# Expert weights in 2 MB loads with four rows per partition; the second expert layer by two experts and both column halves

## The chip, the cores and the metric

The kernel runs on one core of one Trainium2 chip. Its time is the device time of one execution in microseconds (us), and lower is better. The engines are PE (TensorE, matrix products; its weight loads are PEld), DVE (VectorE), ACT (ScalarE), POOL (GpSimd) and SP (SyncE, which issues nearly all transfers here). Everything is float32.

## The reference

Two residual blocks on 256 tokens of width 1024. The first has four half-step feed-forward layers, two mixers and two gated projections. The second has an attention-like mixer and an expert layer, twice:

```
x = x + g1 * mixer(norm(x))                  # layer 0: also for 256 context tokens
h = norm(x) * (1 + sc2) + sh2
aff  = softmax(h @ w_router)                 # 16 experts
gate, idx = top_k(aff.T, 32)                 # each expert picks 32 tokens
xe   = h[idx]                                # 16 x 32 x 1024
hid  = silu(xe @ w1) * (xe @ w3)             # w1, w3, w2: 16 x 1024 x 1024 per layer
ye   = hid @ w2 * gate
x = x + g2 * scatter_add(ye, idx)
```

In layer 0 the same weights serve the tokens and the context, so an expert has 64 rows there, and 32 in layer 1. One expert matrix is 4 MB (MB is 2^20 bytes where it counts loads), so each expert layer reads 3 x 16 x 4 = 192 MB of weights, each byte once.

## The kernel before

Each engine has a program written out by hand, and they meet on semaphores. Only two things set the order around the change.

**The ring.** Weights go through `ring`, twelve slots of 1 MB (128 partitions x 2048 floats). SP's `load` (line 3682) waits until the slot's previous user has been released (`w_used[s]`) and issues one 1 MB transfer. PE's `chunk` waits for `w_in[s]`. `done_with_chunk` only puts the slot on a list: it is released by the next product that PE runs (`mm`, the `held.pop()`), one slot per product. The list matters: the slots of one piece of work come free when the next piece has begun. Loads are issued strictly in the order in which SP's program names them; a wait of one holds up all behind it.

**The expert layers.** `moe(l)` on each engine. Layer 0 works in 8 passes of 2 experts (`groups` = 2, 64 rows each, so a product is 128 x 64 against 128 x 512), layer 1 in 4 passes of 4 experts (`groups` = 4, 32 rows each). A pass multiplies with `w1` (name h1), `w3` (h3) and, after `turn_hidden` has transposed the hidden rows, `w2` (y, run in the next round before that round's h1 and h3); `scatter` adds the previous pass's result to its tokens. `by_weights` does one matrix of a pass: for each quarter q of the 1024 input rows it takes one 1 MB chunk per expert (two rows of 4 KB, so 8 KB, per partition), and for both rows, both column halves and all experts it runs a product; I call the work between two such waits a unit. In layer 0 a unit is 2 chunks (2 MB) and 8 products, in layer 1 it is 4 chunks (4 MB) and 16 products. The first pass of a layer is p; layer 0 then has the written-out rounds a and b, where `gather_quarter` and `gather_x` also gather tokens, and a loop of five more rounds (layer 1: two); the last y is `m0.z.y` or `m1.z.y`.

Some chunks of the first pass do not go through the ring but early into other buffers (`EARLY`: SX, H, AR, XC), as soon as these are free. `ISSUED` gives the order in which layer 0's first loads are issued: with chunks 16 and 17, which belong to m0.a.h1, ahead of the early chunks 13, 14, 7, 12 and 15, whose buffers come free late.

The last unit of `m1.z.y` is cut by column halves (`last_half`): four half chunks for the left half, `add_last(0)`, four for the right half, `add_last(1)`. While `paired(k)` picks every second column of the token rows, it matches the two rows per partition of a chunk.

## Time and profile before

| | us |
|---|---|
| median of 3 runs | 2720.47 |
| the runs | 2719.14 to 2724.95 |
| span of the profiled execution, first to last instruction | 2717.5 |
| PE busy | 2486.2 (91%) |
| DVE busy | 958.0 (35%) |
| ACT busy | 450.6 (17%) |
| chain that ended last, share on PE | 75% |
| chain that ended last, share on DMA | 20%, of it `ring<-moe_w` 19% |

The profiled execution's own device time is not listed beside its span, so the span stands for it: it lies 3.0 us under the median of the runs. The page cuts the span into 40 slices of 68 us. A product in float32 shows as two MATMUL instructions, so x16 in a row of the trace is 8 products. A matmul's duration overlaps that of its neighbours; what counts is the distance between starts.

The second block begins at about 1220 us. The first expert layer's products run from 1602 to 2053 us, the second's from 2274 us to the end.

### The profile page before, as it was taken

Reading aid. Unit: us, or ns where it says so; the run is one execution under the profiler, and the core shown is the slowest. Engines: PE = TensorE matmul, PEld = TensorE weight load, DVE = VectorE, ACT = ScalarE, POOL = GpSimd, SP = SyncE. Lnnn points to the kernel's source line nnn. Section 1 sums busy time; section 2 is a strip of 40 time slices with the busy share of each in tenths; the row PEclk is TensorE's granted clock in tenths of the full one; section 3 lists DMA queues with packets and bytes.
Section 4 is the critical chain, followed back from the end, with each engine's and each line's share of the span. In section 5 each row is a group of like instructions: output and inputs, shape, how many; then the busy total and the mean of one; then the engine's idle time right before and its main releaser. Section 6 shows DMA issues by size and latency. Waiting matters only on the chain.

```text
span 2717.5 us, 26882 instructions
## 1 busy us (share of the span) xinstructions
PE 2486.2 (91%) x10689; PEld 1408.1 (52%) x10689; DVE 958.0 (35%) x1629; ACT 450.6 (17%) x858; POOL 49.3 (2%) x63
## 2 busy tenths in 40 slices
PE   9999999999999999999999999988889998665656
PEld 4546754464548864558876654433335765221213
DVE  5452454555561454552235642111123242000002
ACT  1101311011111221112223420000002131000001
POOL 0000000000000000011000100000000000000000
PEclk9999999999999999999999999999999999888788
DMA  7458663663459564567422279999997328999998
GB/s 281 144 212 277 222 234 137 227 234 126 170 206 300 176 216 140 216 183 158 145 90 76 103 270 407 421 422 422 422 422 257 109 93 343 421 421 422 422 421 350
DMA packets 239078, 700.95 MB, mean 258 GB/s; under 512 B 16952, under 2 KB 126696, under 8 KB 192296
## 3 DMA queue, kind: packets, MB, share of 16 engines
q1 hardware_dynamic: 231776, 686.73, 66.8%
q10 hardware_dynamic: 5088, 8.33, 0.9%
q0 software_dynamic: 2112, 4.46, 0.9%
q8 instruction: 73, 1.20, 0.2%
q14 instruction: 29, 0.24, 0.0%
HBM read 695.30 MB, written 4.06 MB: 257 GB/s over the span
## 4 chain that ended last, share of the span: by engine, by line
PE 75%; DMA 20%; DVE 2%; SPq 1%; issue 1%; ACT 0%; ACTq 0%; POOL 0%; DVEq 0%
PE bank L589 73%; DMA ring<-moe_w 19%; PE bank L598 2%; SPq L3682 1%; DMA ring<-ada_w 0%; ACT AR L3013 0%; DVE AR L1904 0%; DMA AR<-vec 0%; DVE AR L1901 0%; DVE AR L2506 0%; DVE AR L2780 0%; DVE H L1904 0%; DVE AR L2888 0%; DVE AR L2779 0%; DVE XC L1907 0%
## 5 line engine op out<-in xcount | busy, mean ns | idle before, releaser
L589 PE MATMUL bank<-ring,AR 128*32 128x512 f32 (+3 forms) x3656 | 895.9, 665 | 195.8 <-DMA ring<-moe_w 188.6
L589 PEld LDWEIGHTS bank<-ring,AR 128*32 128x32 f32 (+2 forms) x3656 | 329.1, 150 | 716.5 <-issue 685.1
L589 PE MATMUL bank<-H,ring 128*128 128x256 f32 (+3 forms) x2288 | 513.6, 386 | 1.8 <-DVE H L1904 0.8
L589 PEld LDWEIGHTS bank<-H,ring 128*128 128x128 f32 (+2 forms) x2288 | 423.5, 188 | 85.4 <-issue 25.8
L3013 ACT ACTIVATE AR<-bank 128x512 f32<-128x512 f32 (+3 forms) x306 | 174.9, 576 | 1681.8 <-PE bank L589 1108.2
L589 PE MATMUL bank<-AR 128*128 128x512 f32 (+15 forms) x1456 | 402.9, 446 | 15.0 <-DVE AR L2871 6.2
L589 PE MATMUL bank<-ring,H 128*128 128x256 f32 (+3 forms) x1536 | 407.1, 500 | 1.1 <-DVE H L1904 0.6
L1901 DVE TENSOR_TENSOR AR<-AR,bank 128x512 f32<-128x512 f32 (+2 forms) x156 | 97.1, 624 | 763.5 <-PE bank L589 762.3
L589 PEld LDWEIGHTS bank<-ring,H 128*128 128x128 f32 (+1 forms) x1536 | 228.2, 170 | 153.8 <-issue 115.9
L589 PEld LDWEIGHTS bank<-AR 128*128 128x128 f32 (+7 forms) x1456 | 208.8, 184 | 161.7 <-issue 133.6
L1901 DVE TENSOR_TENSOR SX<-ring 128x1024 f32<-128x1024 f32 (+3 forms) x48 | 78.0, 1624 | 287.5 <-PE bank L589 263.6
L589 PE MATMUL bank<-SX,AR 128*128 128x512 f32 (+4 forms) x360 | 135.5, 536 | 2.4 <-ACT SX L3013 2.2
L3013 ACT ACTIVATE AR<-AR 128x512 f32<-128x512 f32 (+7 forms) x156 | 95.2, 637 | 231.5 <-DVE AR L1901 144.4
L598 PEld LDWEIGHTS bank<-cst,AR 128*128 128x128 f32 (+2 forms) x629 | 75.1, 151 | 72.5 <-issue 52.8
L1901 DVE TENSOR_TENSOR AR<-AR 128x256 f32<-128x256 f32 (+8 forms) x180 | 89.6, 526 | 52.2 <-ACT AR L3013 50.0
L598 PE MATMUL bank<-cst,AR 128*128 128x128 f32 (+2 forms) x629 | 98.0, 280 | 4.3 <-DVE AR L1901 1.4
L1913 DVE COPY AR<-bank 128x512 f32<-128x512 f32 (+4 forms) x48 | 29.0, 616 | 174.5 <-PE bank L589 148.6
L589 PEld LDWEIGHTS bank<-SX,AR 128*128 128x128 f32 (+2 forms) x360 | 58.5, 178 | 58.9 <-issue 47.0
L1901 DVE TENSOR_TENSOR ring<-ring,AR 128x1024 f32<-128x1024 f32 (+3 forms) x48 | 77.4, 1618 | 5.0 <-PE bank L589 5.0
L1901 DVE TENSOR_TENSOR ring<-ring 128x1024 f32<-128x1024 f32 (+3 forms) x48 | 77.8, 1620 | 0.5
L1901 DVE TENSOR_TENSOR AR<-ring,SX 128x1024 f32<-128x1024 f32 (+3 forms) x48 | 77.7, 1619 | 0.1
L3013 ACT ACTIVATE AR<-XC 128x512 f32<-128x512 f32 (+1 forms) x76 | 38.5, 535 | 181.1 <-DVE XC L1907 109.1
(145 smaller groups left out, 938.1 us busy)
## 6 DMA issues: line engine op xcount, KB each, us to landing
ring<-moe_w SPq DMA_DIRECT2D x364, 1024.0 KB, 15.2
ring<-ffn_w SPq DMA_DIRECT2D x104, 1024.0 KB, 9.5
ring<-ada_w SPq DMA_DIRECT2D x48, 1024.0 KB, 5.5
ring<-m_w_in SPq DMA_DIRECT2D x26, 1024.0 KB, 11.9
ring<-ffn_w SPq DMA_DIRECT2D x32, 768.0 KB, 7.6
ring<-even_w_in SPq DMA_DIRECT2D x24, 1024.0 KB, 6.4
AR<-moe_w SPq DMA_DIRECT2D x18, 512.0 KB, 7.6
ring<-m_w_out SPq DMA_DIRECT2D x8, 1024.0 KB, 11.5
```

The costliest lines, as they stand in the source:

```text
L589: ins = pe.matmul(o, lhsT, rhs, start=start, stop=stop, skip_group_check=True)
L598: ins = pe.transpose(o, src, ident[0:n, 0:n])
L1901: return dve.tensor_tensor(o, a, b, op)
L1913: dve.tensor_copy(o, v).then_inc(free[b], 1)
L3013: return act.activation(o, i, func, **kw)
L3682: sp.dma_start(v, src).then_inc(w_in[s], 16)
```

## The change

- SP gets `load_pair`: one transfer of 2 MB into two neighbouring slots (an even one and the next), with four rows of 4 KB (16 KB) per partition. It waits for the release of both slots, and signals `w_in` of the even one only. `Ring.pair` skips a slot where the count is odd.
- The loads of w1 and w3 of each layer's first pass stay single 1 MB chunks (and early ones); all later loads of expert weights are pairs, but for the very last.
- Layer 0's first loads: chunks 16 and 17 are now the first pair, behind the early chunks.
- `by_weights` works in units of two experts and four rows: 2 pairs (4 MB), 16 products in both layers. In layer 1 a matrix is four units: experts 0 and 1, both halves of the input rows, then experts 2 and 3. The right column half of an expert goes to the row group two further on (`turned_place`), so that four products in a row lie in four different column groups of the array.
- Because of that, the right half's result rows of layer 1 belong to other experts than the left half's: DVE makes a second set of index and gate columns (`IC`, `GC` 4:8) and a second one-hot `PG[:, nt:2*nt]` per pass, and `scatter` and `add_last` take the one that belongs to their half.
- Rows are permuted by four in place of two: `paired` becomes `fourth` (every fourth column as a product's weights), and the `shift` rows are gathered by 16 small products in place of 4.
- The end of `m1.z.y`: experts 2 and 3 only; two single chunks, then two half chunks for the left half, `add_last(0)`, two for the right.

```diff
 class Ring:
+    def pair(self):
+        self.k += self.k % 2
+        s = self.k % RING
+        self.k += 2
+        n, before = self.uses[s], self.release[s + 1]
+        self.uses[s] += 1
+        self.release[s] = self.release[s + 1] = (s, n + 1)
+        return s, self.count(n), before
...
-        ISSUED = [(*range(7), 8, 9, 10, 11, 16, 17, 13, 14, 7, 12, 15), ()]
+        FIRST = [(*range(7), 8, 9, 10, 11, 13, 14, 7, 12, 15), tuple(range(32))]
...
+            def pair_of_chunks():
+                s, n, _ = loads.pair()
+                pe.wait_ge(w_in[s], 16 * n + 16)
+                held_next.append(s)
+                return ring[:, s:s + 2, :].rearrange("p a (k n) -> p (a k) n", n=D)
...
-                        for r in range(2):
-                            for half in range(2):
-                                mm(bank[b][64 * half:64 * half + 64, 4 * r:4 * r + 4], ident[:, r:P:2],
-                                   MODS[:, 1, 24 + half:32:2, 0], r == 0, True, full[b] if r == 1 and half == 1 else None)
+                        for r in range(4):
+                            for q in range(4):
+                                mm(bank[b][32 * q:32 * q + 32, 2 * r:2 * r + 2], ident[:, r:P:4],
+                                   MODS[:, 1, 24 + q:32:4, 0], r == 0, True, full[b] if r == 3 and q == 3 else None)
...
+                    def turned_place(g, half):
+                        return (g + 2 * half) % groups if l == 1 else g
...
-                            ws = [weights_of_pass(i) for _ in range(groups)]
-                            for kk in range(2):
-                                k = 2 * q + kk
-                                for half in range(2):
-                                    for g, (place, w) in enumerate(ws):
...
+                        units = [(first, q) for first in range(0, groups, 2) for q in range(2)]
+                        for u, (first, q) in enumerate(units):
+                            if between is not None and u in at:
+                                between(*((u,) if len(at) > 1 else ()))
+                            if name == "m1.z.y" and u == 3:
+                                ws = [(None, chunk(2, D)) for _ in range(2)]
+                                for kk in range(2):
+                                    products(4 + kk, ws, kk, first)
+                                for _ in ws:
+                                    done_with_chunk()
                                 for half in range(2):
-                                    last_half(half, b0 + half, left)
+                                    ws = [(None, chunk(2, 512)) for _ in range(2)]
+                                    for kk in range(2):
+                                        products(6 + kk, ws, kk, first, (half,))
+                                    for _ in ws:
+                                        done_with_chunk()
+                                    if half == 0:
+                                        idle_products(5)
+                                        add_last(0)
                                 continue
+                            ws = [(None, pair_of_chunks()) for _ in range(2)]
+                            for kk in range(4):
+                                products(4 * q + kk, ws, kk, first)
+                            for _ in ws:
+                                done_with_chunk()
...
                     def one_hot(n):
+                        if l == 1:
+                            dve.tensor_scalar(PG[:, nt:2 * nt], IOF[:, 0:nt], IC[:, bass.ds(n + 4, 1)], GC[:, bass.ds(n + 4, 1)],
+                                              ALU.is_equal, ALU.mult)
...
+            def load_pair(src):
+                s, n, before = loads.pair()
+                if loads.i is not None or n > 0:
+                    sp.wait_ge(w_used[s], n)
+                if before is not None and before[0] != s:
+                    sp.wait_ge(w_used[before[0]], before[1])
+                sp.dma_start(ring[:, s:s + 2, :].rearrange("p a n -> p (a n)"), src).then_inc(w_in[s], 16)
...
+            first_singles()
+            if l == 0:
+                pairs(1, (0,))
+                pairs(0, (2,))
+                pairs(1, (1, 2))
+                pairs(2, (0, 1, 2))
+            else:
+                pairs(0, (2,))
```

SP's queue where layer 0's expert weights begin, before the change. `w_usedN` is the release of ring slot N; `full2` and `full7` are the waits for the buffers H and AR:

```order
L3682 DMA ring<-moe_w3_2 128x2048 [waits w_used4]
L3682 DMA ring<-moe_w1_2 128x2048 [waits w_used5]
L3682 DMA ring<-moe_w1_2 128x2048 [waits w_used6]
L3752 DMA H<-moe_w3_2 128x1024 [waits full2]
...
L3752 DMA AR<-moe_w3_2 128x4x256 [waits full7]
L3752 DMA AR<-moe_w3_2 128x4x256
L3682 DMA ring<-moe_w1_2 128x2048 [waits w_used7]
L3682 DMA ring<-moe_w1_2 128x2048 [waits w_used8]
L3682 DMA ring<-moe_w1_2 128x2048 [waits w_used9]
```

And now:

```order
L3729 DMA ring<-moe_w3_2 128x2048 [waits w_used4]
L3809 DMA H<-moe_w3_2 128x1024 [waits full2]
...
L3809 DMA AR<-moe_w3_2 128x4x256 [waits full7]
L3809 DMA AR<-moe_w3_2 128x4x256
L3739 DMA ring<-moe_w1_2 128x4096 [waits w_used7,w_used6]
L3739 DMA ring<-moe_w1_2 128x4096 [waits w_used9,w_used8]
L3739 DMA ring<-moe_w1_2 128x4096 [waits w_used11,w_used10]
```

The two chunks that filled slots 5 and 6 ahead of the early ones are gone; slot 5 is skipped, and the first pair needs slot 7, which holds the first chunk of the layer.

PE's queue at m0.a.h1 in layer 0 (x7 stands for seven more products), before:

```order
L589 MATMUL bank<-ring,SX 64x512 [waits w_in5,free1,w_in6,free0,xcur_ready]
L589 MATMUL bank<-ring,SX 64x512 x7
L589 MATMUL bank<-ring,SX 64x512 [waits w_in8,w_in7]
L589 MATMUL bank<-ring,SX 64x512 x7
L598 MATMUL bank<-cst,AR 128x128 [waits free4,free2]
```

And now:

```order
L606 MATMUL bank<-ring,SX 64x512 [waits w_in6,free1,w_in8,free0,xcur_ready]
L606 MATMUL bank<-ring,SX 64x512 x15
L615 MATMUL bank<-cst,AR 128x128 [waits free4,free2]
L615 MATMUL bank<-cst,AR 128x128 x3
L606 MATMUL bank<-ring,SX 64x512 [waits w_in0,w_in10]
```

The boundary in the middle of the sixteen products, at which the first two slots were released, is gone.

PE's queue at the end of the kernel, before:

```order
L589 MATMUL bank<-ring,AR 32x512 [waits w_in4,w_in5,w_in3,w_in2]
L589 MATMUL bank<-ring,AR 32x512 x7
L589 MATMUL bank<-cst 128x2 [waits free5]
L589 MATMUL bank<-cst 128x2 x3
L589 MATMUL bank<-AR 128x512 [waits free6,pg_ready]
L589 MATMUL bank<-AR 128x512
L589 MATMUL bank<-ring,AR 32x512 [waits w_in8,w_in9,w_in7,w_in6]
L589 MATMUL bank<-ring,AR 32x512 x7
L589 MATMUL bank<-AR 128x512 [waits free7,pg_ready]
L589 MATMUL bank<-AR 128x512
```

And now:

```order
L606 MATMUL bank<-ring,AR 32x512 [waits w_in5,w_in4]
L606 MATMUL bank<-ring,AR 32x512 x7
L606 MATMUL bank<-ring,AR 32x512 [waits w_in7,w_in6]
L606 MATMUL bank<-ring,AR 32x512 x3
L606 MATMUL bank<-cst 128x2 [waits free5]
L606 MATMUL bank<-cst 128x2
L606 MATMUL bank<-AR 128x512 [waits free6,pg_ready]
L606 MATMUL bank<-AR 128x512
L606 MATMUL bank<-ring,AR 32x512 [waits w_in9,w_in8]
L606 MATMUL bank<-ring,AR 32x512 x3
L606 MATMUL bank<-AR 128x512 [waits free7,pg_ready]
L606 MATMUL bank<-AR 128x512
```

The left half's result (`bank<-AR 128x512`) now stands between two column halves of 1 MB each, where it stood between two of 2 MB each.

## Rows read from the trace of the kernel before

**Rows 1.** The page: slices of the span, granted clock and DMA rate
```profile
PEclk9999999999999999999999999999999999888788
GB/s 281 144 212 277 222 234 137 227 234 126 170 206 300 176 216 140 216 183 158 145 90 76 103 270 407 421 422 422 422 422 257 109 93 343 421 421 422 422 421 350
```

**Rows 2.** DMA view, four stretches: rows of 1, 2, 4 and 8 KB
```profile
DMA packets 6899, 6.97 MB, mean 349 GB/s; under 512 B 104, under 2 KB 6898, under 8 KB 6898
...
DMA packets 3492, 6.96 MB, mean 387 GB/s; under 512 B 98, under 2 KB 98, under 8 KB 3491
...
DMA packets 763, 2.93 MB, mean 418 GB/s; under 512 B 48, under 2 KB 48, under 8 KB 763
...
DMA packets 13901, 101.25 MB, mean 422 GB/s; under 512 B 1542, under 2 KB 1542, under 8 KB 1542
```

**Rows 3.** Chain of waits, one pass of layer 0: start, us, what
```profile
1847.30 10.72 PE bank L589 x32
...
1883.66 23.19 DMA ring<-moe_w
1906.99 10.72 PE bank L589 x32
```

**Rows 4.** PE in order of time, layer 0 begins, [idle before <- releaser]
```profile
1616.05 7.04 PE L589 MATMUL bank<-ring,AR 128*64 128x512 f32 x32
...
1629.78 7.04 PE L589 MATMUL bank<-ring,SX 128*64 128x512 f32 x32
1636.75 1.23 PE L598 MATMUL bank<-cst,AR 128*128 128x128 f32 x8
```

**Rows 5.** DMA by stretches of layer 0's begin (clock, share, GB/s last)
```profile
1634.00:1635.00 1.00, 1.00 (x8) 0.35 (x6) 0.00 (x0) 0.00 (x0) 0.00 (x0) 1.00 0.10 25
1635.00:1636.00 1.00, 1.00 (x8) 0.36 (x6) 0.00 (x0) 0.00 (x0) 0.00 (x0) 1.00 0.73 131
...
1640.00:1680.00 40.00, 40.00 (x192) 16.01 (x189) 8.18 (x9) 2.39 (x4) 0.00 (x0) 1.00 1.01 422
```

**Rows 6.** PE in order of time, end of round b, gather_x, next y
```profile
1727.99 3.65 PE L589 MATMUL bank<-ring,AR 128*64 128x512 f32 x16 [1.31 <-DMA ring<-moe_w]
1731.57 7.13 PE L589 MATMUL bank<-AR 128*128 128x512 f32 x16
1738.55 1.11 PE L598 MATMUL bank<-cst,AR 128*128 128x128 f32 x8
1739.50 7.08 PE L589 MATMUL bank<-AR 128*128 128x256 f32 x32
1746.51 28.98 PE L589 MATMUL bank<-ring,AR 128*64 128x512 f32 x134
```

**Rows 7.** PE in order of time, end of layer 0
```profile
2026.30 3.65 PE L589 MATMUL bank<-ring,AR 128*64 128x512 f32 x16 [1.32 <-DMA ring<-moe_w]
2029.89 7.13 PE L589 MATMUL bank<-AR 128*128 128x512 f32 x16
...
2038.80 13.96 PE L589 MATMUL bank<-ring,AR 128*64 128x512 f32 x64 [0.83 <-ACT AR L3013]
```

**Rows 8.** PE in order of time, layer 1
```profile
2397.31 5.34 PE L589 MATMUL bank<-ring,AR 128*32 128x512 f32 x32 [4.59 <-DMA ring<-moe_w]
```

**Rows 9.** PE in order of time, the kernel's end
```profile
2700.86 1.92 PE L589 MATMUL bank<-ring,AR 128*32 128x512 f32 x16 [1.77 <-DMA ring<-moe_w]
2702.71 1.05 PE L589 MATMUL bank<-cst 128*128 128x2 f32 x8
2703.75 1.96 PE L589 MATMUL bank<-AR 128*128 128x512 f32 x4
2706.11 1.92 PE L589 MATMUL bank<-ring,AR 128*32 128x512 f32 x16 [0.41 <-DMA ring<-moe_w]
```

**Rows 10.** PE in order of time, the shift products, about 1217 us
```profile
1216.59 0.41 PE L589 MATMUL bank<-MODS,cst 128*64 128x4 f32 x8
1216.93 5.23 PE L589 MATMUL bank<-H,ring 128*128 128x256 f32 x23
```

More of the change, by code:

```diff
@@ L146, in __init__, with count @@
         self.k, self.uses, self.i, self.per = 0, [0] * RING, None, 1
+        self.release = [None] * RING
+    def count(self, n):
+        return n if self.i is None else n + self.per * self.i
     def next(self):
@@ L150, in next @@
         self.k += 1
-        n = self.uses[s]
+        n, before = self.uses[s], self.release[s]
         self.uses[s] += 1
-        return s, (n if self.i is None else n + self.per * self.i)
+        self.release[s] = (s, n + 1)
+        return s, self.count(n), before
[6 more added lines that the diff above has]
+        self.release[s] = self.release[s + 1] = (s, n + 1)
+        return s, self.count(n), before
     def loop(self, i, per=1):
@@ L160, in end @@
         self.i = None
-        self.uses = [u + self.per * (rounds - 1) for u in self.uses]
+        for s in range(0, RING, 2):
+            self.uses[s] += self.per * (rounds - 1)
+            self.release[s] = self.release[s + 1] = (s, self.uses[s])
 def two_blocks(nc, T, out):
@@ L621, in chunk @@
             def chunk(*dims):
-                s, n = loads.next()
+                s, n, _ = loads.next()
                 pe.wait_ge(w_in[s], 16 * n + 16)
@@ L756, in p1 @@
                 def p1(g):
-                    loaded[f, "up", g] = [(s, 16 * n + 16) for s, n in (loads.next() for _ in range(4))]
+                    loaded[f, "up", g] = [(s, 16 * n + 16) for s, n, _ in (loads.next() for _ in range(4))]
                     arrive(loaded[f, "up", g][0])
@@ L864, in down @@
                         if n == 1:
-                            loaded[f, "down", j] = [(s, 16 * c + 16) for s, c in (loads.next() for _ in range(2))]
+                            loaded[f, "down", j] = [(s, 16 * c + 16) for s, c, _ in (loads.next() for _ in range(2))]
                         lo, hi = loaded[f, "down", j]
@@ L1735, in last_half @@
-                    def last_half(half, b, left):
-                        ws = [last_weights() for _ in range(groups)]
-                        for kk in range(2):
-                            for g, w in enumerate(ws):
-                                at = (6 + kk) * P + g * slots
-                                mm(bank[b][slots * g:slots * (g + 1), :], left[:, at:at + slots], w[:, kk, :], False, kk == 1,
-                                   full[b] if kk == 1 and g == groups - 1 else None)
-                        for _ in ws:
-                            done_with_chunk()
-                        if half == 0:
-                            idle_products(5)
-                            add_last(0)
+                        single = name in (f"m{l}.p.h1", f"m{l}.p.h3")
@@ new lines, in products @@
+                        def products(k, ws, row, first, halves_=(0, 1)):
+                            for half in halves_:
+                                b = b0 + half
+                                for g, (place, w) in enumerate(ws, first):
+                                    if place is not None:
+                                        rhs = early_half(place, row, half)
+                                    elif w.shape[2] == D:
+                                        rhs = w[:, row, half * 512:(half + 1) * 512]
+                                    else:
+                                        rhs = w[:, row, :]
+                                    o, c = turned_place(g, half), turned_place(g, int(left is HIDT and k >= 4))
+                                    mm(bank[b][slots * o:slots * (o + 1), :], left[:, k * P + c * slots:k * P + (c + 1) * slots],
+                                       rhs, k == 0, k == KT - 1,
+                                       full[b] if k == KT - 1 and g == groups - 1 else None)
@@ new lines, in by_weights @@
+                        if single:
+                            for q in range(4):
+                                ws = [weights_of_pass(i) for _ in range(groups)]
+                                for kk in range(2):
+                                    products(2 * q + kk, ws, kk, 0)
+                                for place, _ in ws:
+                                    if place is None:
+                                        done_with_chunk()
+                            return
+                        units = [(first, q) for first in range(0, groups, 2) for q in range(2)]
@@ L3767, in first_passes, with rows_of @@
-                    def first_passes():
-                        uses = straight()
-                        for n in ISSUED[l] + tuple(n for n in range(len(uses)) if n not in ISSUED[l]):
-                            at, part = uses[n]
-                            w, q, g = parts()[part]
+                    quads = [T[name][l].rearrange("e (q p k) n -> e q p k n", p=P, k=4) for name in
+                             ("moe_w1_2", "moe_w3_2", "moe_w2_2")]
+                    def rows_of(n, w, q, g):
+                        return quads[w][n * groups + g, q // 2][:, 2 * (q % 2):2 * (q % 2) + 2, :]
@@ new lines, in single_parts, with load_quad, pairs @@
+                    def single_parts(ws):
+                        return [(w, q, g) for w in ws for q in range(4) for g in range(groups)]
+                    def load_quad(n, w, q, g):
+                        if type(n) is int:
+                            load_pair(quads[w][n * groups + g, q].rearrange("p k n -> p (k n)"))
+                        else:
+                            load_pair(quads[w][bass.ds(n * groups + g, 1), q].rearrange("a p k n -> (a p) (k n)"))
+                    def pairs(n, ws, units=groups):
+                        for w in ws:
+                            for u in range(units):
+                                for g in range(2):
+                                    load_quad(n, w, u % 2, u // 2 * 2 + g)
```

92 lines of the change are left out of this document (39 added, 53 removed).

## The prediction

> **What bounds the kernel now.** I read the slices first [rows 1]: in the first 24 of the 40 slices the DMA rate wanders between 76 and 300 GB/s, and PE is busy for 91% of the whole; the change touches little there. In slices 26 to 30 and 35 to 39 the rate sits at 421 to 422 GB/s and does not move. Those are the two expert layers, and a flat rate like that is a full queue. The chain of waits says the same [rows 3]: in the steady passes of layer 0 the last unit of one pass starts at 1847.30 and that of the next at 1906.99, so 59.69 us for 24 MB of weights, 2.487 us per MB, and what PE follows is a load issued 23.19 us earlier. In PE's order of time layer 1 is DMA-bound too: a unit takes 5.34 us and waits 4.59 us for weights before it [rows 8]. So in both layers three things count: how fast the bytes come, whether the queue ever runs dry, and what PE still has to do after the last byte.
>
> **How fast 16 KB rows come.** The DMA view has four stretches with a full queue and one row size each [rows 2]: 349 GB/s at 1 KB, 387 at 2 KB, 418 at 4 KB, 422 at 8 KB. With 16 engines a row takes size x 16 / rate: 46.9, 84.7, 156.8 and 310.6 ns. A line through the first and the last has a slope of 0.0368 ns per byte and 9.2 ns that each row pays once; at 2 KB it gives 84.6 where 84.7 was measured. By it a 16 KB row takes 612.0 ns where two of 8 KB take 621.2: 1.5% less, 428 GB/s, 2.450 us per MB, 0.037 us saved per MB. The bounds: nothing saved (621.2), and the 9.2 ns and all else above the bare slope of 2 to 4 KB gone, about 603 ns (435 GB/s, 0.073 us per MB). The step from 4 to 8 KB alone gives 618.2 ns, 0.012 us per MB. I take the line, since three of four sizes lie on it.
>
> The pairs that lie in DMA-bound stretches: in layer 0 all 192 MB but the 28 chunks up to the first slot stall (below) and the last 8, whose products PE reaches later than they land: 156 MB. In layer 1 16 + 96 + 44 = 156 MB. Each 156 x 0.037 = 5.8 us, together -11.5 us.
>
> The Trainium skill, DMA: Bandwidth & Descriptors, section "Why small descriptors are slow (HBM only)", gives a fixed cost of about 3 cycles per packet. With the 850 MHz of the same page that is an estimate of 3.5 ns, where the rows' line has 9.2; the saving would be 4.4 us in place of 11.5 and the time 2727.6. The same page's fit for one DMA (2.0 us fixed plus bytes at 436 GB/s) would have 1 MB take 4.4 us; the trace disagrees, 2.487 us, because twelve loads are queued, so the halved number of loads earns nothing of that 2 us here.
>
> **What the coarser grain costs in layer 0.** Four terms, each read where PE and the queue meet.
>
> First, the slot stall at 1633. PE runs a.h1 from 1629.78 [rows 4]; with twelve slots full the queue goes dry, the rate drops to 25 and 131 GB/s, and is back at 422 from about 1635.7 on [rows 5]. What ends it is the release of chunks 16 and 17 at the unit boundary 3.43 us after 1629.78 (half of the 6.97 us to 1636.75), at 1633.2; so 2.5 us lie between a boundary and flowing data. Afterwards the boundary is behind 16 products, at 1636.75, and the pair that holds 16 and 17 is released there: the same bytes flow from 1639.2. From here on the queue is full in both kernels until PE catches up, so these 3.5 us stay. That 16 and 17 are no longer loaded ahead of the early chunks, and that slot 5 is skipped for a lap, costs nothing more: the first pair issues at about 1606.9 with slot 7's release and lands some 15 us before PE needs it at 1629.8. +3.5 us.
>
> Second, gather_x. When the last unit of round b has landed, the ring has 4 MB just landed, and 8 MB outstanding after its start (4, and the 4 released by it); 4 more are issued when it ends. That is 12 x 2.450 = 29.4 us of data. The next release comes when the y unit after next begins: 6.9 (unit) + 14.9 (scatter, turn, gather_x, 1731.57 to 1746.51) + 6.9 + 2.5 = 31.2 us [rows 6]. The queue is dry for 1.9 us. Before, a unit and its follower were 3.4 us each, 24.3 us, and it never was. In an ordinary pass gather_x's 7.0 us are missing and a wait of 0.8 is added: 25.0 us against 29.4, no stall. +1.9 us.
>
> Third, the end of the layer. The last h3 unit is followed by scatter, turn and y without a wait for weights [rows 7], so PE ends there by its own work after the last h3 bytes. That unit is 6.9 us in place of 3.5. +3.4 us. Both y units have landed by then: 19.6 us of data against 22.7 us until the second starts.
>
> Fourth, everything else in layer 0 lies beside DMA waits of 1.3 us per 2 MB, which become about 2.9 us per 4 MB.
>
> **Layer 1.** A unit was 4 MB and 16 products, and stays so; the slots held are the same, and the skipped slot 3 leaves at least 3 MB outstanding. Four neighbouring products are in four column groups before and after. The second one-hot (0.3 to 0.4 us of DVE per pass) and eight small index copies go into PE's 4.6 us of wait; without that cover they would cost 1 us each.
>
> The end changes [rows 9]. Before, the left half's products start at 2700.86, its result at 2703.75, done when the right half lands at 2706.11: 5.25 us between the halves for 2 MB. Now 1 MB lies between, about 2.6 us. PE needs for the left half 1.85 + 1.04 + 1.96 = 4.85 us from its landing, so the right half's products start 2.2 us after its landing and not 0.1. Half as many bytes come in 2 KB rows: -0.4 us. +1.7 us.
>
> **Elsewhere.** 16 shift products in place of 4, in a stretch where PE is never idle: 8 instructions took 0.34 us from start to start, 24 more take 1.0 [rows 10]; bounds 0.4 (half as wide) and 4.8 (0.2 us each, nothing overlapping). The gathers' weights at a stride of four: I cost them at nothing, since the transposes at stride two run at the pace of the others; bounds 0 and 2 us. +1.0 us.
>
> **Sum.** -11.5 + 3.5 + 1.9 + 3.4 + 1.7 + 1.0 = 0.0. The span stays at 2717.5; with the 3.0 us between it and the median of the runs, the forecast is 2720.5 us.
>
> **Rivals.**
> - Nothing saved per row (the DMA engines cut 16 KB into two of 8, so the change doesn't do what it says; the number of packets would tell). Then -11.5 falls away and the dry stretch is 1.5: 2731.6. For it: from 4 to 8 KB the rate rose by only 1%. Against: the line fits 8 KB.
> - Little saved per row (618.2 ns, or the smaller fixed cost that the skill's page states): 156 x 2 x 0.012 = 3.8 saved, 2728.2.
> - PE's clock in layer 0. Its waits were 1.3 us and the granted clock 10 tenths; in layer 1 waits of 4.6 us went with 7 to 8 tenths and units of 5.3 us for 3.6 us of work [rows 1, 8]. The new waits of 2.9 us lie between. If they cost the clock in the same proportion, a unit is 10.1 us, above its 9.8 us of data: the last unit, the unit at gather_x, and the slot stall each lose 3.2 us or part of it, 2727. It decides from about 9.8 us per unit. Against: the busy share stays at 70%, where layer 1's is 54.
> - More saved: the row's fixed part shrinks further (603 ns, 156 x 2 x 0.073 = 22.8), 2709; or the saving is as forecast and the slot stall and the dry stretch don't bite, 2715 or a little under.
>
> **How the numbers follow.** Forecast 0.42 (its own range 2715 to 2726); more saved or less lost 0.32; nothing saved 0.11; little saved 0.08; clock 0.07. A measurement of this kernel can tell 0.2%, 5.4 us, from no change. So faster 0.32, same 0.42, slower 0.26. The range leaves out the far end of more saved and little else: 2710 to 2732.
>
> **What would show it.** Right: rate in the expert layers near 428 GB/s with some 21,000 packets of 16 KB; a steady pass of layer 0 near 58.8 us; a dip in the rate near 1637 and near 1757; scatter at the end of layer 0 about 6.9 us after its last unit starts; the last unit's products beginning about 2 us behind their landing. Wrong: 422 GB/s still; PE's clock below 10 tenths in layer 0; dips in every pass; or no dip anywhere, which would mean that my account of when slots come free is too strict.

## The result, and the profile after

The changed kernel takes 2736.32 us (median of 5 runs, 2734.9 to 2737.0), the kernel before 2720.47: a ratio of 1.0055, 95% interval 1.0044 to 1.0066. It is 15.9 us slower; the forecast was no change, 2720.5, with a range of 2710 to 2732. The profiled execution has a span of 2735.2 us against 2717.5, 17.7 more; 1.2 us of that is there before the first changed instruction of PE (the shift products start at 1217.78 and not at 1216.59), and executions of one kernel differ by as much.

The rates first. The slices of the page after, which answer to [rows 1]:

```profile
PEclk9999999999999999999999999999999999777878
GB/s 279 141 213 276 223 237 139 218 237 117 170 225 282 185 200 154 213 184 150 152 79 91 98 257 404 400 422 428 429 421 245 108 91 319 419 427 426 428 428 335
DMA packets 214374, 700.94 MB, mean 256 GB/s; under 512 B 14264, under 2 KB 124008, under 8 KB 188584
```

The packets of the kernel before:

```profile
DMA packets 239078, 700.95 MB, mean 258 GB/s; under 512 B 16952, under 2 KB 126696, under 8 KB 192296
```

Where nothing disturbs it (slices 28, 29 and 36 to 39), the full queue now runs at 426 to 428 or 429 GB/s, where it ran at 421 to 422: the forecast of 428 held. Packets of 8 KB and more fell from 46,782 to 25,790, so the 16 KB rows are whole packets. But slice 26 (1710 to 1778 us), at 421 before, is at 400, and slice 27 at 422. Something starves the queue there. The chain of waits shows a steady pass of layer 0 (start, us, what), to be read beside [rows 3]:

```profile
1860.35 14.15 PE bank L606 x48
...
1919.12 14.15 PE bank L606 x48
```

From 1860.35 to 1919.12 are 58.77 us for 24 MB, 2.449 us per MB. Before it was 59.69; the forecast was near 58.8. So each steady pass gains what was expected, and yet the layer ends later. PE in order of time where it begins, of the kernel before and of the kernel after (start, us, what, [idle before <- releaser]); the 32 instructions, 16 products, gather the first tokens:

```profile
1597.11 4.04 PE L589 MATMUL bank<-AR 128*128 128x128 f32 x32 [1.09 <-DVE AR L1904]
```
```profile
1598.58 7.74 PE L606 MATMUL bank<-AR 128*128 128x128 f32 x32 [1.10 <-DVE AR L1944]
```

An instruction took 0.13 us and now takes 0.24. The weight loads alone, same stretch, before and after:

```profile
1597.11 3.85 PEld L589 LDWEIGHTS bank<-AR 128*128 128x128 f32 x32 [1.29 <-DVE AR L1904]
```
```profile
1598.57 7.54 PEld L606 LDWEIGHTS bank<-AR 128*128 128x128 f32 x32 [1.29 <-DVE AR L1944]
```

The products are as wide as before; it is loading the weights, 128 columns now 16 bytes apart instead of 8, that doubled.

PE's clock is not the cause, though it fell here: in the gather after the change the granted clock was 0.50, the lower of its two levels (1.2 GHz), from 1598.5 to 1601.9 and 1.00 (2.4 GHz) from then on, and the weight loads followed each other every 0.23 us on both sides. At the old spacing the clock does matter. In an execution of before_late (below), where it fell for as long in the same gather, the weight loads came every 0.12 us at the higher level and every 0.21 us at the lower, and the gather took 5.57 us. So the new spacing costs 3.7 us where the clock would have stayed up, and 2.2 where it fell, as it did in the first gather of layer 1 before the change (0.72 from 2267 to 2273), here before and after:

```profile
2267.59 5.56 PE L589 MATMUL bank<-AR 128*128 128x128 f32 x32 [0.89 <-DVE AR L1904]
```
```profile
2282.37 7.73 PE L606 MATMUL bank<-AR 128*128 128x128 f32 x32 [0.89 <-DVE AR L1944]
```

The first products on expert weights follow the gathers, and with them the first release of a ring slot. SP's queue, before and after (start, us, the DMAs that it issued):

```profile
1567.78 19.44 SPq L3682 DMA_DIRECT2D ring<-moe_w  x3
1588.91 1.75 SPq L3752 DMA_DIRECT2D H<-moe_w  x4
1594.30 2.88 SPq L3752 DMA_DIRECT2D AR<-moe_w  x6
1606.85 31.25 SPq L3682 DMA_DIRECT2D ring<-moe_w  x14
```
```profile
1560.88 8.65 SPq L3729 DMA_DIRECT2D ring<-moe_w  x2
1590.37 2.84 SPq L3809 DMA_DIRECT2D H<-moe_w  x4
1595.87 3.84 SPq L3809 DMA_DIRECT2D AR<-moe_w  x6
1612.07 17.95 SPq L3739 DMA_DIRECT2D ring<-moe_w  x6
```

The first pair issues at 1612.07, not near 1606.9 as the prediction had it, and between 1595.87 + 3.84 and then nothing is issued. Of the 5.2 us by which this issue is later than before, 1.5 were there when the gather began and 3.7 are the gather. The windows of both executions (stretch, length, PE busy, granted clock, DMA share, GB/s), before and after:

```profile
1580.00:1600.00 20.00, 17.09 (x88) 1.00 0.65 241
1600.00:1620.00 20.00, 20.00 (x100) 1.00 0.88 342
1620.00:1640.00 20.00, 20.00 (x98) 1.00 0.91 368
1640.00:1660.00 20.00, 20.00 (x99) 1.00 1.01 423
```
```profile
1580.00:1600.00 20.00, 17.20 (x75) 0.96 0.44 145
1600.00:1620.00 20.00, 20.00 (x94) 0.95 0.71 260
1620.00:1640.00 20.00, 20.00 (x96) 1.00 1.00 428
1640.00:1660.00 20.00, 19.47 (x94) 1.00 0.99 403
...
1608.00:1610.00 2.00, 2.00 (x12) 1.00 0.02 6
1610.00:1612.00 2.00, 2.00 (x12) 1.00 0.00 0
...
1760.00:1780.00 20.00, 20.00 (x96) 1.00 0.81 329
```

The four stretches lack 96 + 82 - 60 + 20 = 138 GB/s x 20 us = 2.8 MB, 6.4 us at 428 GB/s. The queue stands empty around 1610, in place of the stall at 1633 [rows 5], which is gone (1620 to 1640 is full): PE is later, and what was on its way has landed before PE releases slot 7. A second hole lies at the gather of the other tokens: 0.19 of 20 us, 3.8 us, where the forecast had 1.9 and the kernel before none.

The end of layer 0, which answers to [rows 7]:

```profile
2037.67 7.09 PE L606 MATMUL bank<-ring,AR 128*64 128x512 f32 x32 [1.11 <-DMA ring<-moe_w]
2044.69 7.13 PE L606 MATMUL bank<-AR 128*128 128x512 f32 x16
2053.60 6.66 PE L606 MATMUL bank<-ring,AR 128*64 128x512 f32 x30 [0.83 <-ACT AR L3060]
```

The last h3 unit starts 11.4 us later than before, and the scatter follows it after 7.0 us instead of 3.6: the forecast's +3.4. The y unit starts 14.8 us later. Layer 1 adds 2.2 us in its own first gather, shown above. The kernel's end, which answers to [rows 9]:

```profile
2718.28 1.91 PE L606 MATMUL bank<-ring,AR 128*32 128x512 f32 x8 [0.62 <-DMA ring<-moe_w]
...
2721.13 1.96 PE L606 MATMUL bank<-AR 128*128 128x512 f32 x4 [0.41 <-DVE AR L1941]
2723.02 1.91 PE L606 MATMUL bank<-ring,AR 128*32 128x512 f32 x8
```

The right half's products (2723.02) now wait for no load; they stand behind the left half's result on PE, as forecast.

### The profile page after: what moved, and what is told of

Read it like the earlier page. It is cut to its first block, busy times and chain, and to the rows that moved or that the text cites. A ratio compares the mean times of both kernels' runs of the same rounds, so it can differ in the third digit from the quotient of the medians.

```text
span 2735.2 us, 26558 instructions
## 1 busy us (share of the span) xinstructions
PE 2516.6 (92%) x10709; PEld 1435.4 (52%) x10709; DVE 958.2 (35%) x1641; ACT 449.9 (16%) x858; POOL 49.3 (2%) x63
## 4 chain that ended last, share of the span: by engine, by line
PE 77%; DMA 19%; DVE 2%; issue 1%; SPq 1%; ACT 0%; ACTq 0%; DVEq 0%; POOL 0%
PE bank L606 75%; DMA ring<-moe_w 18%; PE bank L615 2%; DMA ring<-ada_w 0%; SPq L3739 0%; ACT AR L3060 0%; DVE AR L1941 0%; DVE AR L1944 0%; DMA AR<-vec 0%; DVE AR L2546 0%; DVE AR L2935 0%; DVE AR L2820 0%; DVE H L1944 0%; DVE AR L2819 0%; SPq L3729 0%
## 5 line engine op out<-in xcount | busy, mean ns | idle before, releaser
L606 PE MATMUL bank<-ring,AR 128*32 128x512 f32 (+3 forms) x3656 | 905.2, 671 | 180.9 <-DMA ring<-moe_w 173.7
L606 PE MATMUL bank<-AR 128*128 128x512 f32 (+15 forms) x1456 | 424.7, 462 | 16.4 <-DVE AR L2915 7.2
L606 PEld LDWEIGHTS bank<-AR 128*128 128x128 f32 (+7 forms) x1456 | 232.7, 204 | 158.9 <-issue 126.8
L615 PEld LDWEIGHTS bank<-cst,AR 128*128 128x128 f32 (+2 forms) x629 | 75.0, 150 | 73.0 <-issue 53.0
L615 PE MATMUL bank<-cst,AR 128*128 128x128 f32 (+2 forms) x629 | 98.0, 280 | 4.6 <-DVE AR L1941 1.7
L1941 DVE TENSOR_TENSOR ring<-ring 128x1024 f32<-128x1024 f32 (+3 forms) x48 | 77.7, 1620 | 0.5
L3060 ACT ACTIVATE AR<-bank,AR 128x512 f32<-128x512 f32 (+3 forms) x96 | 51.6, 556 | 104.5 <-PE bank L606 57.6
```

The costliest lines, as they stand in the source:

```text
L606: ins = pe.matmul(o, lhsT, rhs, start=start, stop=stop, skip_group_check=True)
L615: ins = pe.transpose(o, src, ident[0:n, 0:n])
L1941: return dve.tensor_tensor(o, a, b, op)
L3060: return act.activation(o, i, func, **kw)
```

## The experiments

Each kernel but the last two ran 7 to 11 times, beside 19 to 33 runs of the kernel before (median 2721.2 in the first set, 2720.4 in the second, 2720.3 in the third). A ratio is to the kernel before of the same set; its interval is about 0.0009 to either side, 2.5 us, so a difference between two medians of less than that is weak by itself; where the ratios say something else than the medians, both stand.

**One: which part costs.** The theory was the weight loads' spacing and the coarser grain of layer 0 together; the rivals were each alone, and slower copies.

before_stride4, the kernel before with the gathers' weights at every fourth column (the gathered values are then not the reference's):

```
+ def every_fourth(k): return slice(k // 4 * 4 * P + k % 4, (k // 4 + 1) * 4 * P, 4)
- mm(bank[b][:, :], TM[:, 2 * s + t, paired(k)], PM[:, 2 * s + t, :], ...
+ mm(bank[b][:, :], TM[:, 2 * s + t, every_fourth(k)], PM[:, 2 * s + t, :], ...     (and in the three other gathers)
```


> The kernel before, with one edit: the products that gather tokens take every fourth column of the token rows as their weights, where they took every second (so they gather the rows in another order than the loads need). Loads and units are those of before. Theory S (stride): a 128-column weight load whose columns lie 16 bytes apart takes about 0.24 us where 8 bytes apart it takes 0.12, as the 32 instructions of a gather took 7.74 us after the change and 4.04 before. Then this kernel alone is slower: the first gather of layer 0 delays the layer by 3.7 us, that of layer 1 by 2.2 to 3.7 us, the second gather_quarter and gather_x lie beside a full queue; 2726 to 2729 us (+6 to +8). Rival G (grain): the gathers are slow after the change for another reason (they stand beside 2 MB loads), and this kernel stays within 2 us of before.

Measured 2726.99, ratio 1.0021 (1.0012 to 1.0030): +5.8 us with no other change.

after_contig, the changed kernel with the token rows written in the order in which the gathers read them, so that their weights are contiguous:

```
- TM[:, 2 * s + t, fourth(k)]
+ TM[:, 2 * s + t, k * P:(k + 1) * P]
- take(f"tm{l}...", TM[:, 2 * s + t, g * 512:(g + 1) * 512], lambda b: b[:, :])
+ take(f"tm{l}...", TM[...].rearrange("p (r c) -> p r c", r=4), lambda b: b[:, :].rearrange("p (c r) -> p r c", r=4))
```


> The changed kernel, with one edit: the token rows are written to SBUF in the order in which the gathers read them (the copies from PSUM read at a stride of four), so that every gather's weights are 128 neighbouring columns. Theory S: the gathers are back at 4.0 us per 32 instructions or less, the queue's dry stretches of 6.0 us at the start of layer 0 and of 7.4 us at the start of layer 1 shrink by about 3.7 us each, and the time is about 2728 us (-8), still slower than before by the coarse grain in layer 0. Rival G: the time stays at 2736. Rival W: the stride moves to the copies, each of which takes twice as long in the router's chain, and gives back some 2 to 4 us: 2731 to 2734.

Measured 2728.73, ratio to the kernel before 1.0021 (1.0012 to 1.0030), 7.6 us less than the changed kernel (9 by the two ratios). The copies that now reorder keep their time (0.59 us on ACT, 0.69 on DVE).

before_contig, the same edit on the kernel before:

> The kernel before, with the same edit: the token rows are written in gathering order, and the gathers' weights are 128 neighbouring columns in place of every second one. It tells a stride of two from one. Theory S with a step at 16 bytes (two weights per 16 bytes are free): within 2 us of before, 2718 to 2722. Rival: the cost is proportional to the stride, so a stride of two already costs half of what four costs: the gather's 32 instructions fall from 4.04 to below 3 us and the time by 2 to 4 us.

Measured 2719.42, ratio 0.9994 (0.9985 to 1.0003): 8 bytes apart costs nothing that can be measured against contiguous; 16 bytes does.

layer0_undone, after_contig with layer 0 back in 1 MB loads and units of 2 MB, chunks 16 and 17 ahead again; layer 1 keeps its pairs:

```
- single = name in (f"m{l}.p.h1", f"m{l}.p.h3")
+ single = l == 0 or name in (f"m{l}.p.h1", f"m{l}.p.h3")
...
- pairs(1, (0,)); pairs(0, (2,)); pairs(1, (1, 2)); pairs(2, (0, 1, 2))
+ single_pass(...)      # load(rows_of(n, w, q, g), 2, D) for each q, g
```


> The changed kernel with contiguous gathers, and with layer 0 put back: 1 MB loads, units of 2 MB, chunks 16 and 17 ahead of the early ones, as before; layer 1 and the end keep the pairs. Theory L0 (the coarse grain of layer 0 costs more than its faster rows save, layer 1 gains): against the changed kernel with contiguous gathers, layer 0 gives back about 8 us (3.4 for the last unit, 3.9 dry at gather_x, some 5 for two chunks fewer ahead, minus 5.8), so about 2718 to 2720; against before, layer 1 gives -5.8 + 1.8 + 0.3. Rival: layer 1 loses as well (its weights' rate is not what ends the wait): 2722 or more.

Measured 2718.31, ratio 0.9984 (0.9975 to 0.9993). So four kernels form a ladder: 2719.4 (before, contiguous), 2718.3 with layer 1's pairs, 2728.7 with layer 0's too, 2736.3 with the weights at a stride of four: -1.1, +10.4, +7.6 (by the ratios -3, +10, +9).

**Two: where layer 0's 10.4 us go.** All on contiguous weights.

ahead, on after_contig: the ring starts at slot 1, so that no slot is skipped, and the first pair of pass 1 is loaded ahead of early chunk 13:

```
- self.k, self.uses, self.i, self.per = 0, [0] * RING, None, 1
+ self.k, self.uses, self.i, self.per = 1, [0] * RING, None, 1
...
+ if l == 0 and n == 13:
+     load_quad(1, 0, 0, 0)
...
```


> The token-contiguous version of the changed kernel (2728.7 us) with the 2 MB loads of layer 0's pass 1 started one pair earlier, ahead of the early layer's last chunk, so that no slot is skipped. Theory G (layer 0's coarser grain costs because the queue runs dry where the ring's slots come free late: 4.5 us at 1609): about 2 MB more is on its way when the gathers begin, the dry stretch at 1609 falls from 4.5 us to 0 to 2, the kernel takes 2724 to 2726. Rival C (the time goes in the clock and the units, not in the queue): the dry stretch shortens but the kernel stays at 2728 to 2730.

Measured 2726.5 (ratio 1.0019, 1.0010 to 1.0028): 2.2 less by the medians, 0.5 by the ratios: inconclusive by its time. SP now issues a pair at 1588.49, and around 1606 the queue is fuller (0.83 against 0.59 in after_contig), but then the stall of the prediction appears, later than before; windows of ahead:

```profile
1606.00:1616.00 10.00, 10.00 (x50) 1.00 0.83 292
1630.00:1640.00 10.00, 10.00 (x49) 1.00 0.58 248
```

What the earlier pair wins is lost again, in part at least, where the ring is full.

gatherx, on after_contig: the other tokens' gather stands between y and h1 of round b and not behind the round:

```
  by_weights(f"{pre}y", 6, HIDT, i)
...
+ if pre == "m0.b.":
+     gather_x((0, 1, 2, 3))
```


> The token-contiguous version of the changed kernel (2728.7 us) with the 7 us of the other tokens' transposes in layer 0 moved one round earlier, to between y and h1 of round b, where the ring stands fuller. Theory G: the queue's dry stretch of 3.8 us at 1765 goes or becomes under 1 us, the kernel takes 2725 to 2726. Rival M (the stretch only moves to where the transposes now stand): a dry stretch of 3 to 4 us near 1745 and 2728 to 2730.

Measured 2724.85 (ratio 1.0011, 1.0002 to 1.0020): 3.9 less (2.7 by the ratios), for a hole of 3.8. The stretch after_contig's queue lost, and gatherx's, at the old and the new place of the gather:

```profile
1760.00:1780.00 20.00, 19.73 (x94) 1.00 0.81 329
```
```profile
1760.00:1780.00 20.00, 17.43 (x76) 0.91 1.00 428
1700.00:1720.00 20.00, 20.00 (x94) 1.00 1.01 424
```

The rival, that the hole moves with the gather, fell.

tail4, on layer0_undone: the last y of the kernel in single experts, 1 MB loads and two halves of four experts, as before the change:

> The version with layer 0 in 1 MB loads and layer 1 in pairs (2718.3 us), with the very last layer of the kernel (m1.z.y) back in single experts, 1 MB loads and halves of the last chunk as before the change. Prediction's term for the kernel's end (+1.7 us): the last products start 0.1 instead of 2.2 us after the last landing, and the kernel takes 2716 to 2717. Rival: the smaller rows of the last 12 MB give part of it back (about 0.04 us per MB, and less at rows of 1 and 2 KB): 2718 to 2719.

Measured 2716.31 (ratio 0.9976, 0.9965 to 0.9987). That is 2.0 under layer0_undone, and 4.0 under the kernel before (6.5 by the ratio): the fastest of all that ran. PE in order of time at the end of tail4:

```profile
2703.42 1.92 PE L611 MATMUL bank<-ring,AR 128*32 128x512 f32 x16 [0.40 <-DMA ring<-moe_w]
```

PE waits for the last load again. The 2.0 us agree with the prediction's +1.7 for the new end, though they are less than the interval.

three, the edits of ahead, gatherx and tail4 together on after_contig:

> All three edits (earlier first pair, the other tokens' transposes one round earlier, the last layer in single experts) on the token-contiguous version of the changed kernel. Theory G: the savings add, 3 + 3 + 1.5 us, and give 2720 to 2722, against 2718.3 for layer 0 in 1 MB loads; what is left over is the last h3 unit of layer 0 (3.4 us). Rival C (clock and units): 2725 to 2728, more than half of layer 0's 10 us remains though the queue no longer runs dry.

Measured 2720.13 (ratio 0.9994, 0.9985 to 1.0003): 8.6 less than after_contig (7.3 by the ratios); the single edits sum to 8.1 (5.4 by the ratios). Against tail4 (1 MB loads in layer 0, all else alike) 3.8 us are left. Windows of three and of tail4 around the slot stall:

```profile
1604.00:1616.00 12.00, 12.00 (x58) 1.00 0.99 370
...
1632.00:1644.00 12.00, 12.00 (x60) 1.00 0.57 218
```
```profile
1632.00:1644.00 12.00, 12.00 (x60) 1.00 0.85 328
```

With nothing starving the queue earlier, the stall stands where the prediction put it, and in this window it is 12 x (0.85 - 0.57) = 3.4 us longer than with 1 MB loads; 3.5 were forecast. But tail4's queue starves earlier instead (a share of 0.73 from 1604 to 1616), and over 1604 to 1644 the two move the same, 348 and 346 GB/s. So the stall has the forecast size, and these runs do not show that it costs the layer as much.

**Three: the order of the loads, and the weight load.** I had costed the loss of chunks 16 and 17 ahead of the early ones at nothing; the small gain of ahead made me doubt it.

before_late and before_both:

```
- ISSUED = [(*range(7), 8, 9, 10, 11, 16, 17, 13, 14, 7, 12, 15), ()]
+ ISSUED = [(*range(7), 8, 9, 10, 11, 13, 14, 7, 12, 15, 16, 17), ()]      (before_both: and every_fourth as above)
```


> The kernel before with weight chunks 16 and 17 of layer 0 loaded behind the early chunks, as in the changed kernel, and nothing else changed. The prediction's sentence that this costs nothing more: 2720 to 2721. Theory G (in a layer where the DMA queue sets the pace, 2 MB that are not on their way at 1587 are missing until its end): 2 MB x 2.487 us = 5.0 us less the 1.9 us of the stall at 1634, which then finds the ring less full: +3 us, 2723 to 2724.

> The kernel before with the gathers' weights at every fourth column (its result is then not the reference's) and chunks 16 and 17 loaded behind the early chunks. If the two costs add: 5.8 measured for the columns alone plus 3, 2729 to 2730. If the ring, less full at the gathers, runs dry for longer as they take 3.7 us more: the same 2729 to 2730 or a little more. If 16 and 17 cost nothing: 2727.

Measured 2720.78 (ratio 1.0006, 0.9997 to 1.0015) and 2726.74 (1.0025, 1.0016 to 1.0035). The later theory fell, and the half of the prediction's sentence that is on chunks 16 and 17 stands: their order alone costs nothing that can be measured, with fast weight loads or slow ones. SP's queue of before_late, and its windows, show why:

```profile
1597.69 41.55 SPq L3682 DMA_DIRECT2D ring<-moe_w  x16
```
```profile
1606.00:1616.00 10.00, 10.00 (x50) 1.00 1.02 418
```

The two slots are still free, the 1 MB loads go out at 1597.69 as soon as the early ones are issued, and fill the hole that the kernel before has at 1606. In the changed kernel a pair needs two neighbouring slots, and slot 5 is skipped: nothing can be issued until PE releases slot 7, at 1612.07 (at 1606.92 in three, where the gather took 3.84 us). So the hole comes from the grain and not from the order.

stride8 and stride3, every eighth and every third column on the kernel before (again not the reference's values):

> The kernel before with the gathers' weights at every eighth column, 32 bytes apart (its result is then not the reference's). Known: 8 bytes apart 4.04 us for 32 of the 128x128 products, 16 bytes apart 7.74. If a weight load's time goes with the bytes that it spans: 15 us for 32. If it has one slower pace beyond 8 bytes: 7.7 us again.

> The kernel before with the gathers' weights at every third column, 12 bytes apart (its result is then not the reference's). If the time goes with the bytes spanned, from 4.04 us at 8 bytes and 7.74 at 16: between, about 5.8 us for 32. If only power-of-two spacings or distances of 16 bytes are slow: 4.0. If everything over 8 bytes is slow: 7.7.

Each ran once, 2732.5 and 2724.6 us; single runs, of which only the gathers are read here. The first gather in stride8, in stride3, and, contiguous, in three:

```profile
1602.23 7.91 PE L592 MATMUL bank<-AR 128*128 128x128 f32 x32 [1.09 <-DVE AR L1907]
```
```profile
1599.39 6.46 PE L592 MATMUL bank<-AR 128*128 128x128 f32 x32 [1.09 <-DVE AR L1907]
```
```profile
1597.38 3.84 PE L606 MATMUL bank<-AR 128*128 128x128 f32 x32 [1.09 <-DVE AR L1956]
```

These times are not all of one clock. In three and in the kernel before it stayed up in this gather; in stride3 it was at its lower level from 1600.4 to 1603.8. Read from the distance between two weight loads at the higher level, the pace is 0.11 us at 4 bytes, 0.12 at 8, 0.175 at 12, 0.23 at 16 and 0.24 at 32. It rises between 8 and 16 bytes, then stays: neither simple rule fits. The Trainium skill's "SBUF Cachelines" (Advanced Engine Details and Errata) fits all five: two or more elements per 16-byte line are fast, one per line is slow, and at 12 bytes, where four elements lie in three lines, the time is half as long again as at 8. (The transposes do not follow it; see the last section.) The Trainium skill's page SBUF — State Buffer, section "Door 1: The DMA port swizzle (why `[64,N]` ≈ `[32,N]`)", reads the same rule as a free stride of up to 4 for fp32; the 0.23 us at 16 bytes disagree.

## Why the prediction was wrong

Two steps failed. By the ladder of medians the gathers' weights, forecast at nothing, cost 7.6 us, and layer 0's larger loads and units, forecast at 3.0, cost 10.4. Either miss alone would have left the time inside the range (2728.1 and 2727.9 us).

**The step that failed first** is "The gathers' weights at a stride of four: I cost them at nothing, since the transposes at stride two run at the pace of the others; bounds 0 and 2 us." Alone it costs 5.8 us, within the change 7.6. The row I leant on was at stride two, and nothing in the trace showed stride four. It was also of the wrong instruction: after the change the transposes, too, take their weights at a stride of four, and they run at the same pace as before (1.11 us for eight, last section). It is the weight loads of products that slowed. The distance from two to four was taken as the distance from one to two. Such a bound should have been a weight load twice as long (3.7 us at each of two exposed gathers, 7.4 us); that was the number to put into the range. It also has its effect at a place where the whole DMA-bound layer waits: the first release of a slot hangs behind the first gather.

The Trainium skill had the rule, and I did not weigh it: Advanced Engine Details and Errata, section "SBUF Cachelines", says that SBUF is read in lines of 16 bytes and that an access keeps its pace only if at least two neighbouring elements fall into one line. The measured 4.04 us at 8 bytes (two a line) and 7.74 at 16 (one a line) agree with it; the transposes, whose weights at 16 bytes cost nothing more, do not.

**Layer 0's grain was mis-sized.** The forecast was -5.8 + 3.5 + 1.9 + 3.4 = +3.0; measured, with contiguous weights, +10.4. Term by term:
- Slot stall, +3.5: it has that size in three (3.4), but there it is no loss against 1 MB loads over the whole begin of the layer (348 against 346 GB/s), so that the numbers agree is in part luck. In the changed kernel the queue starved earlier, and this stall did not come. "That slot 5 is skipped for a lap, costs nothing more" looked at the wrong thing: I asked when PE needs the pair ("some 15 us before"), and in a stretch that the queue bounds the question is whether the queue has work; it had none from 1608 to 1612. What that cost is not settled: the ahead edit gave back between 0.5 and 2.2.
- gather_x, +1.9: the hole was 3.8, and its removal brought 3.9 (2.7 by the ratios). So the queue had work for 2 us less than my count of 12 MB on their way behind the last unit of the round; where the count is wrong is not shown.
- Last h3 unit, +3.4: right, read at 2037.67.
- What is left, 10.4 - 2.2 - 3.9 = 4.3 by difference of the medians, stands against -5.8 + 3.5 + 3.4 = +1.1. Those 3 us are not settled and are hardly beyond the intervals. PE's clock, below, is of that size.

**PE's clock** (the rival at 0.07) did come in part, and below the bound at which the rival was to decide. Many units of layer 0 now follow waits of 2.0 to 3.0 us. Some of these still took 7.09 us, others 8.4 to 8.8; here one in the changed kernel, and a longer one, of 10.08 us, in after_contig:

```profile
1977.88 8.50 PE L606 MATMUL bank<-ring,AR 128*64 128x512 f32 x32 [2.79 <-DMA ring<-moe_w]
```
```profile
1858.71 10.08 PE L606 MATMUL bank<-ring,AR 128*64 128x512 f32 x32 [2.80 <-DMA ring<-moe_w]
```

The granted clock from 1660 to 2020 was 1.00 in every window of 40 us before, and 0.96 to 1.00 after (down to 0.94 in after_contig). By the rival's bound a unit shorter than its 9.8 us of data costs nothing. That holds in the middle of a pass: after the unit at 1850.47, which took 8.78 us, the queue stayed full (430 GB/s from 1850 to 1870). It does not hold for the last unit of a pass, behind which the next slot comes free only with the second unit of the next y. After such a unit of 7.09 us (1860.35) and after the one of 8.50, in the changed kernel, and after the one of 10.08, in after_contig:

```profile
1860.00:1900.00 40.00, 36.39 (x155) 1.00 1.01 428
1980.00:2020.00 40.00, 37.14 (x158) 0.99 1.00 415
```
```profile
1860.00:1900.00 40.00, 37.63 (x150) 0.94 0.95 391
```

The same goes for the other profiled executions with 4 MB units: 406 to 416 GB/s after a last unit of 8.78 us, and, away from the gather of the other tokens, 423 to 429 after all but one of 7.09 (418, in ahead). With 2 MB units (the kernel before, layer0_undone) the clock stays at 1.00 and the rate at 420 to 423 throughout. From these rates I estimate 1.2 us (415 against 428 GB/s over 40 us) to 3.5 us (391) for each slow last unit, about 2 us for the two in the changed kernel's profiled execution and 5.5 for the two in after_contig's. So the 4.4 us of slack that the prediction counted in an ordinary pass (29.4 against 25.0) are nearly all missing, and the clock may well be the open 3 us. No run held the clock fixed, so its share of the medians stays open.

**Layer 1.** Forecast -5.8 for the rows and +1.7 for the end. The rate rose from 422 to 428 over 360 us (before_contig, tail4), which is 5 us; in the medians tail4 gains 3.1 over before_contig (4.9 by the ratios), and the change's end takes 2.0 of it back. That is the forecast within what these runs can tell.

**Right:** the rate, 428 GB/s to the GB/s, and with it the fall of both rivals of less saving; the steady pass (58.77); the longer last unit of layer 0 and the order of work at the kernel's end. The 16 shift products (32 instructions) take 0.66 us, and what follows starts 0.25 us later behind their start than before, not the 1.0 forecast:

```profile
1217.78 0.66 PE L606 MATMUL bank<-MODS,cst 128*32 128x2 f32 x32
1218.37 3.94 PE L606 MATMUL bank<-H,ring 128*128 128x256 f32 x17
```

The Trainium skill, DMA: Bandwidth & Descriptors, section "Why small descriptors are slow (HBM only)", with its smaller fixed cost per packet would, by the prediction's estimate, have given less than half of the gain in rate; the measured 428 GB/s goes with the rows' 9.2 ns. The fit for one DMA that the prediction takes from the same page is given there for transfers issued by GpSimd, and these loads are issued by SP.

Two slips in the prediction's working change no term of its sum. Half of 6.97 us is 3.49, not 3.43. And 603 ns is not the slope from 2 to 4 KB but that of the line through the first and the last size (0.0368 ns x 16384); the slope from 2 to 4 KB would give 577 ns, so the bound of more saved lay closer than its words say. Of the "three of four sizes" on that line two were used to draw it.

## What to carry to other kernels

A layout change for the DMA's sake changes the stride at which another engine reads: look for each reader, and where the trace has no row of that instruction at that stride, take a pace twice as slow as a bound, the more so where a queue's first release hangs behind it. In a stretch that a queue bounds, ask of each moved or enlarged load not when its consumer needs it but whether the queue has work meanwhile; twice the grain in layer 0 with the same ring brought 6 us by rate by the prediction's own working and was 10.4 us slower, so it lost some 16, to late releases, to longer last units and, as argued above, in part to the clock. Use larger loads where the consumer has slack (here layer 1, with the end kept fine-grained and the gathers' weights contiguous: 4 us under the kernel before) and keep the small ones where it has none.

## What was not expected of the hardware

- Weight loads of 128x128 f32 products followed each other, at the higher clock, every 0.11 us with their columns 4 bytes apart, 0.12 at 8, 0.175 at 12, 0.23 at 16 and 0.24 at 32. At the lower clock it was 0.21 us at 4, 8 and 12 bytes, and at 16 and 32 the same as at the higher.
- The transposes did not slow down. Their data are their weights: where the data are 16 columns wide, L615's weight load is 128x16 and its moving side 128x128. In the expert layers these columns went from 8 to 16 bytes apart, yet eight transposes took 1.11 us before [rows 6] and after, and seven of their weight loads 0.92 us both times; the gather behind them went from 7.08 to 7.72. Why a transpose is spared is open.

```profile
1751.02 1.11 PE L615 MATMUL bank<-cst,AR 128*128 128x128 f32 x8
1751.97 7.72 PE L606 MATMUL bank<-AR 128*128 128x256 f32 x32
```
- The granted clock fell during some gathers, with the old spacing too: the 32 instructions that took 4.04 us in the kernel before took 5.57 in before_late, where the window 1600 to 1616 has a granted clock of 0.96. At 16 bytes the first gathers of both layers took 7.73 or 7.74 us in all three kernels that read every fourth column (the changed one, before_stride4, before_both), wherever the clock fell.
